# A hybrid retention and short-conv block on eight cores: prefix rows staged in an idle buffer, row norms in three steps, and an accumulation begun earlier

## The reference, cut to what matters

```
u = rmsnorm(x) * norm1_w * (1 + sc1) + sh1            # sh1, sc1, g1, ... from silu(c) @ w_ada + b_ada
q, k, v, og, cb, cc, cx, ga, gb = split(u @ w_in)
kh = rotary(k) / sqrt(128)
state_h = sum over earlier rows  gamma_h^(distance) * outer(k_row, v_row)      # retention, 4 heads
y_ret  = (silu(og) * groupnorm(retention(q, k, v))) @ w_ret_out
y_conv = (cb * causal_conv3(cc * cx)) @ w_conv_out
h = x + g1 * ((sigmoid(ga) * y_ret + sigmoid(gb) * y_conv) @ w_o)
out = rmsnorm(h + g2 * (relu(u2 @ w_ff1)^2 @ w_ff2))  # u2: second norm, as u
```

## Time and profile before

| | us |
|---|---|
| time, median of 3 runs (range) | 1362.46 (1361.74 to 1363.98) |
| the profiled execution's own time | 1362.84 |
| its span on the slowest core, core 3 | 1361.3 |
| spans of the eight cores | 1350.7 to 1361.3 |
| PE busy, share of the span | 1236.1, 91% |
| first group of the convolution branch begins (core 3) | 175.6 |

### The profile page before, as it was taken

One profiled execution on the slowest core, in us unless ns is written; L12 is line 12 of the kernel. 1 busy time (PEld: TensorE's weight loads), 2 busy tenths in 40 slices (PEclk: granted clock), 3 DMA queues, 4 the chain that ended last, 5 costly groups with the idle time before them and its releaser, 6 DMA issues.

```text
span 1361.3 us, 18923 instructions; the slowest of 8 cores (1350.7 to 1361.3 us)
## 1 busy us (share of the span) xinstructions
PE 1236.1 (91%) x6288; PEld 582.1 (43%) x6288; DVE 480.3 (35%) x907; ACT 421.1 (31%) x714; POOL 499.8 (37%) x513
## 2 busy tenths in 40 slices
PE   2467799999999999986999999599999999999997
PEld 0233354444444554543444444254444444444443
DVE  5345366766322366664002233260000252000045
ACT  1346143222211266666331112154330023331011
POOL 1155310000000377777653362126661125664012
PEclk8688899999999999997999999799999999999999
DMA  9779270240731500005447927987545449954423
GB/s 171 173 164 193 55 94 1 41 54 1 93 39 24 78 1 1 1 1 76 59 60 110 172 36 158 221 241 124 79 77 81 82 155 169 134 93 64 68 75 135
DMA packets 86591, 124.33 MB, mean 91 GB/s; under 512 B 4704, under 2 KB 69216, under 8 KB 86496
## 3 DMA queue, kind: packets, MB, share of 16 engines
q0 software_dynamic: 67632, 70.26, 37.5%
q1 hardware_dynamic: 16560, 44.48, 10.0%
q10 hardware_dynamic: 2304, 8.39, 1.8%
HBM read 176.59 MB, written 16.78 MB: 142 GB/s over the span
## 4 chain that ended last, share of the span: by engine, by line
PE 84%; DMA 7%; DVE 3%; POOL 2%; issue 2%; another core or an unknown queue 1%; ACT 1%; DVEq 0%; POOLq 0%; SPq 0%; ACTq 0%
PE PS L304 81%; DMA ring<-w_ada 3%; DMA h1s<-scr 2%; DMA scr<-brow 2%; PE PS L450 1%; DMA scr<-x_main 1%; DVE scr L871 1%; DVE scr L529 1%; PE PS L933 1%; DVE scr L527 0%; POOL ring L236 0%; POOL G_t L924 0%; POOL Z L555 0%; PE PS L858 0%
## 5 line engine op out<-in xcount | busy, mean ns | idle before, releaser
L304 PE MATMUL PS<-X,ring 128*128 128x512 bf16 x2560 | 568.3, 381 | 0.0
L304 PEld LDWEIGHTS PS<-X,ring 128*128 128x128 bf16 x2560 | 250.3, 98 | 300.8 <-issue 6.2
L304 PE MATMUL PS<-ring,Z 128*128 128x512 bf16 x896 | 212.5, 393 | 46.2 <-DVE G_t L422 14.7
L304 PEld LDWEIGHTS PS<-ring,Z 128*128 128x128 bf16 x896 | 88.7, 100 | 158.5 <-issue 64.1
L304 PE MATMUL PS<-Y,ring 128*128 128x512 bf16 x512 | 119.0, 379 | 1.8 <-DVE scr L765 1.8
L1116 ACT ACTIVATE scr<-PS 128x512 f32<-128x512 f32 x128 | 76.4, 597 | 140.8 <-PE PS L304 87.5
L304 PE MATMUL PS<-ring,X 128*128 128x512 bf16 x512 | 117.8, 379 | 0.0
L1135 DVE TENSOR_TENSOR AR<-PS,G_t 128x512 f32<-128x512 f32 x16 | 11.1, 692 | 295.1 <-PE PS L304 295.1
L304 PE MATMUL PS<-ring,Y 128*128 128x512 bf16 x512 | 113.4, 379 | 0.0
L757 ACT ACTIVATE scr<-PS 128x512 f32<-128x512 f32 x64 | 38.2, 597 | 187.4 <-PE PS L304 184.5
L236 POOL DMA_DIRECT2D ring<-w_in x17 | 16.7, 983 | 189.8 <-PE PS L304 189.8
(11 more groups left out here) (150 smaller groups left out, 1299.6 us busy)
## 6 DMA issues: line engine op xcount, KB each, us to landing
ring<-w_ff POOLq DMA_DIRECT2D x32, 1024.0 KB, 8.7
ring<-w_in POOLq DMA_DIRECT2D x17, 1024.0 KB, 22.6
scr<-x_main SPq DMA_DIRECT2D x32, 512.0 KB, 10.0
ring<-w_ada POOLq DMA_DIRECT2D x12, 1024.0 KB, 21.0
scr<-x_pre SPq DMA_DIRECT2D x16, 512.0 KB, 15.6
h1s<-scr SPq DMA_DIRECT2D x16, 512.0 KB, 7.3
scr<-h1s SPq DMA_DIRECT2D x32, 256.0 KB, 4.2
y<-scr ACTq DMA_DIRECT2D x16, 512.0 KB, 3.8
```

Of the source, the lines that this page charges most:

```text
L304: S.op("pe", lambda e: e.matmul(out, lhsT, rhs, start=start, stop=stop), reads=list(lkeys) + list(rkeys), writes=[okey])
```

## The change

- **Staging.** The first 6 tiles go to `scr0` to `scr5` as before. Tiles 6 to 13 go to the eight rows of X, which hold nothing yet (rows 0 to 3 had held the temporaries of the sine tables). From tile 14 on it is `scr` again.
- **Gates and order of the loads.** All prefix pairs come first, then all own pairs. Pair 2 waits for the fourth w_ada chunk (before: the third); pairs 3 to 7 are issued together, gated by the landing of the k weights. Behind them each scaling step issues one own pair.
- **Norms in three steps.** `pair_do(0)` squares, `pair_do(1)` variance and power, `pair_do(2)` scales; in the loop a pair's steps stand in three successive turns.
- **The loop** has 16 turns. Transposes are spread one or two calls to a turn; chunks 5, 6 and 7 are let go at t = 4, 8, 12 (before 2, 5, 8).
- **The tail.** Blocks 4 and 5 of M are begun in banks 2 and 3 with tiles 0 to 11, before the last tiles of `kd` are needed; the column sums come later; blocks 6 and 7 go last. The six evictions stand together behind the last norms.
- **O_load** no longer calls `load_x`: it takes `scr[t % 6]`. The counter of `load_x` stood at 32, so that before it began with `scr2`.

```
         def load_x(src, t, gate=()):
-            xi = xbuf["n"] % 6
+            i = xbuf["n"]
             xbuf["n"] += 1
-            dma("sp", scr[xi][:, :], src[t * 128:(t + 1) * 128, :], list(gate), SK(xi), ("xt", xi))
-            return xi
+            ap, keys = x_stage(i)          # X[:, (i - 2) % 8, :] for 6 <= i < 14, else scr
+            dma("sp", ap, src[t * 128:(t + 1) * 128, :], list(gate), keys, ("xt", i % 14))
+            return ap, keys
...
-        pairs = [("p", t) for t in range(0, 12, 2)] + [("m", 0), ("p", 12), ("m", 2), ("p", 14)] + [("m", t) for t in range(4, 16, 2)]
+        pairs = [("p", t) for t in range(0, 16, 2)] + [("m", t) for t in range(0, 16, 2)]
...
+        def pair_do(stage):
+            kind, t = pairs[n_next[stage]]
+            n_next[stage] += 1
+            (x_sq, x_rs, x_sc)[stage](kind, t)
+            if stage == 2 and n_next[2] + 2 > 7:
+                pair_load()
...
         s_wk, k_wk = ring_use()
+        for n in range(5):
+            pair_load([k_wk])
...
+        sq_at = (0, 1, 3, 4, 5, 6, 7, 9, 10, 12, 13)
+        for t in range(16):
+            p_k(t)
+            if n_next[2] < n_next[1]:
+                pair_do(2)
+            if n_next[1] < n_next[0]:
+                pair_do(1)
             if t >= 4:
                 p_m(t - 4, range(4), MA)
+            for kp in {2: (0, 1), 3: (2, 3), 5: (0,), 6: (1,), 7: (2, 3)}.get(t, ()):
+                p_tpart(1 if t < 4 else 2, kp, 2 + kp % 2, "act")
+            if g == 2:
+                p_tpart(3, i, 2, "act")
+            if t in sq_at:
+                pair_do(0)
+            if 10 <= t < 14:
+                m_tpart(0, t - 10, 3, "dve")
+            elif t >= 14:
+                for kp in (2 * t - 28, 2 * t - 27):
+                    m_tpart(1, kp, 2 + kp % 2, "dve" if kp % 2 else "act")
...
+        for t in range(12):
+            p_m(t, [4], [2])
+        norm_tail()
+        p_m(12, range(4), MA)
+        for t in range(12):
+            p_m(t, [5], [3])
+        norm_tail()
+        for t in range(13, 16):
+            p_m(t, range(4), MA)
+        for k, b in ((4, 2), (5, 3)):
+            for t in range(12, 16):
+                p_m(t, [k], [b])
...
         def O_load(t):
-            o_x[t] = load_x(x_main, t)
+            i = t % 6
+            dma("sp", scr[i][:, :], x_main[t * 128:(t + 1) * 128, :], [], SK(i), ("xt", i))
+            o_x[t] = i
```

More of the change, by code:

```diff
@@ L490, in x_load, with x_dst, x_src, x_sq @@
             x_of[kind, t] = load_x(x_pre if kind == "p" else x_main, t, gate)
-        def x_norm(kind, t):
+        def x_dst(kind, u):
+            return (xs_pre(u), xs_preK(u)) if kind == "p" else (mxs(u), mxsK(u))
+        def x_src(kind, u):
+            ap, keys = x_of[kind, u]
+            return (ap if kind == "p" else halves(ap)), keys
+        def x_sq(kind, t):
             col = t if kind == "p" else 16 + t
             for u in (t, t + 1):
-                xi = x_of[kind, u]
-                if kind == "p":
-                    sq_stats(scr[xi][:, :], SK(xi), xs_pre(u), xs_preK(u), col + u - t)
-                else:
-                    sq_stats(halves(scr[xi][:, :]), SK(xi), mxs(u), mxsK(u), col + u - t)
-            rs_stats(col, 2)
-            for u in (t, t + 1):
-                xi = x_of[kind, u]
-                if kind == "p":
-                    scale_x(scr[xi][:, :], SK(xi), xs_pre(u), xs_preK(u), col + u - t)
-                else:
-                    scale_x(halves(scr[xi][:, :]), SK(xi), mxs(u), mxsK(u), col + u - t)
+                src, sk_ = x_src(kind, u)
+                dst, dk = x_dst(kind, u)
+                sq_stats(src, sk_, dst, dk, col + u - t)
+        def x_rs(kind, t):
+            rs_stats(t if kind == "p" else 16 + t, 2)
+        def x_sc(kind, t):
+            col = t if kind == "p" else 16 + t
+            for u in (t, t + 1):
+                src, sk_ = x_src(kind, u)
+                dst, dk = x_dst(kind, u)
+                scale_x(src, sk_, dst, dk, col + u - t)
         def uT_ap(g, k):
@@ L627, in build_program @@
         ring_rel(k_wk)
-        for t in range(16):
-            mm(pa[0], ("pa", 0), ones_bf[:, :], ["ones"], kd_ap[t], [kd_key[t]], t == 0, t == 15)
         kbar = scr[6][:, 0:512]
-        S.op("act", lambda e: e.copy(out=kbar, in_=pa[0]), reads=[("pa", 0)], writes=[SH(6, 0)])
         MT = [scr[7 + k // 4][:, (k % 4) * 256:(k % 4 + 1) * 256].bitcast(BF16) for k in R8]
@@ L640, in m_evict, with norm_tail @@
                  reads=[("pa", b), SH(6, 1), ("mT", 0)], writes=[MTk[k]])
-        for k in range(4):
-            m_evict(k, MA[k])
-        MB = [1, 2, 3, 0]
-        for k in range(4):
+        def norm_tail():
+            if n_next[0] < len(pairs):
+                pair_do(0)
+            if n_next[1] < n_next[0]:
+                pair_do(1)
+            if n_next[2] < n_next[1]:
+                pair_do(2)
+        for t in range(12):
[10 more added lines that the diff above has]
+                p_m(t, [k], [b])
+        for t in range(16):
+            mm(pa[0], ("pa", 0), ones_bf[:, :], ["ones"], kd_ap[t], [kd_key[t]], t == 0, t == 15)
+        S.op("act", lambda e: e.copy(out=kbar, in_=pa[0]), reads=[("pa", 0)], writes=[SH(6, 0)])
+        norm_tail()
+        for k in range(6):
+            m_evict(k, (MA + [2, 3])[k])
+        for k, b in ((6, 1), (7, 0)):
             for t in range(16):
-                p_m(t, [4 + k], [MB[k]])
-            m_evict(4 + k, MB[k])
-            if k < 2:
-                pair_norm()
+                p_m(t, [k], [b])
+            m_evict(k, b)
+        while n_next[2] < len(pairs):
+            norm_tail()
         ring_open(len(chunks))
```

42 lines of the change are left out of this document (18 added, 24 removed).

## The result

| | before | after |
|---|---|---|
| median, us (range) | 1363.22 (1361.74 to 1365.47) | 1354.55 (1354.03 to 1355.31) |
| span of the slowest core | 1361.3 (core 3) | 1352.9 (core 4) |
| first `uTh` matmul there | 174.00 | 160.97 |
| from it to the output projection | 651.6 | 653.0 |
| the output projection until its last matmul | 82.2 | 85.4 |

The ratio is 0.9935 (95% 0.9918 to 0.9953): faster, by 8.7 us and not by the 29.5 forecast, and outside the range. On the slowest core 13.0 us are gained in the prelude, 1.4 lost behind it and 3.2 in the output projection; the rest, 453.5 us, is the same to 0.3.

What follows compares the result with a forecast made beforehand. The prelude was taken as bound by a chain of small waits and a late-starting DMA stream, not one full engine. Span 1361.3 - 33.7 (prelude) + 4 (output projection) = 1331.6 us; forecast 1333, range 1320 to 1349.

Steps and rivals of the forecast that it cites:

- The start: Prelude: k weights land at 48.5 us (bounds 46 and 52) for 59.35; `p_k(4)` starts at 65 for 77.08, gain 12.
- six tiles less are 12.3 us: Loads before the k weights: two prefix tiles beside them for eight, so 59.35 becomes 47.1 us.
- The pace: Loop of the k product: 3.4 us a turn where nothing is late; DVE's 3.7 us power wait removed at no new cost.
- the two stalls: Evictions behind own-row squares: `p_k(8)` at 83 to 84 for 78.6, `p_k(12)` at 102 for 97.
- The own rows: Loop's end: pair 13 lands at 114, squared at 116, PE free at 119; their stream a hair behind PE as next bound.
- rival C: Prelude: own rows' stream late, idle gaps or each late pair one chunk later; 1340 to 1348 us, chance 0.25.
- The tail: Before the convolution branch: 96 matmuls at 0.215 remain, 20.6 us; the branch starts at 140.3 for 174.00.
- 24 stand ahead, 5.2 us of the gain: Tail: of the 84 matmuls that stood behind the last decays, 24 now stand ahead, worth 5.2 us.
- The output projection: First load at about 827.4 us for 755.96; delay passes down stores, loads and `brow`: 4 us lost, bounds 0 and 16.
- Rival E: Prelude: only the start is gained (11 us), POOL and ACT eating the rest; 1355 us, chance 0.04.
- rival B: DMA in the prelude: x tiles flow beside chunks from the start, 10 us more gained; 1323 us, chance 0.2.
- the two signs of being wrong: Prelude: squares of prefix tiles wait past 72 us, or a chunk lands more than 30 us after its issue.

Runs made afterwards that it cites:

- run 9: Staging undone alone in the changed kernel (tiles through the six scratch buffers; three-step norms, loop and early blocks kept): 1361.8 us, ratio 1.001 to the kernel before.
- runs 4 and 6: Each against the changed kernel: 4 puts the three norm steps in one turn, 1360.3 us; 6 leaves out POOL's two rotation additions per k tile, 1347.2 us.
- Run 13: Changed kernel with old O_load order, masks and third chunk behind own rows, no early blocks; own tiles 8 to 15 load 128 of 1024 columns: 1337.9 us.
- run 15: Changed kernel with old O_load order, late masks, no early blocks, and the second chunk opened at turn 12, not 8: 1335.3, 1337.6 and 1342.6 us.
- Run 3: Changed kernel with own tiles 8 to 15 loading 128 of 1024 columns in the prelude: 1355.8 us in the profiled execution, cores 2 and 3 at clock 0.81.
- run 7: Changed kernel with the loads of kdec, qdec and mask and the third chunk opening put behind the own rows: 1347.6 us, ratio 0.990 to the kernel before.
- run 5: The changed kernel again, unedited, on another chip: 1352.3 us, ratio 0.993 to the kernel before.
- run 8: Changed kernel with blocks 4 and 5 of M not begun early: 1348.4 us, ratio 0.990 to the kernel before.
- run 1: Changed kernel with O_load on the buffers of before (scr2 first): 1359.9 us on the first chip, 1345.9 and 1348.3 on a second.

## Why the prediction was wrong

The direction and the places were right, the sizes weren't. Two steps failed, the pace of the turns and the landing of the own rows from tile 8 on; the start and the tail were mis-sized.

- **The start** ("48.5", "gain 12"): right in kind, 3.6 us late for the k weights (0.1 outside the bounds of 46 and 52), and the gain at `p_k(4)` is 4.8 (72.3 for 77.1) and not 12. The three steps take the wait for the power off DVE, not off PE: the transposes of group 1 wait 5.09 us for pair 3's scaling, whose power still stands on POOL behind two tiles' rotation. I had that scaling at 60; it ran from 64.15. The term "six tiles less are 12.3 us" isn't borne out either: without the staging the k weights come 2 us later (run 9).
- **The pace** ("turns go at 3.4 us", "at no new cost"): this step failed. The scaling, which had run while POOL was idle, now runs beside POOL's work, and each slows the other (runs 4 and 6): a turn takes 4.4 us. How much of the extra 1.0 is due to this and how much to the order of DVE's queue isn't priced; without POOL's two sums it is 4.1. The miss isn't seen at `p_k(12)`, which is late by 6.1 only, because the two stalls that I had put at `p_k(8)` and `p_k(12)` didn't come: no own row was waited for before 109. The first four own tiles, issued at 59 to 60, had landed by 77 when chunk 5 was issued, at 80.33 and not at 72, and the next four landed 5 us after their issue. Two errors offset each other there, which is luck. Run 13 shows the pace nearly bare: from the start of `p_k(4)` to that of `p_k(15)` 71.7 to 120.5 (medians), 4.4 us a turn with 3 to 5 us of late rows in all, where eleven turns at 3.4 are 37.
- **The own rows** (rival C, "1340 to 1348"): the step that failed most, 10.6 us between `p_k(12)` and the end of `p_k(15)`. Tiles 8 and 9, for which the sum had no wait, were issued just behind the second chunk and waited for 10.1 and 3.5 us; run 15 shows that the chunk does it. I had pair 13 (tiles 10 and 11) issued at 99, landed at 114 and squared at 116; it was issued from 111.55 on, since the scaling that frees its buffers came at the slower pace, and squared at 130.59 and 132.59, beside the third chunk and the mask. Run 3 prices the late rows at 10 us, run 7 chunk and three loads at 5.6 of them (median `uTh` 151.5 for 157.1 in run 5). This is the mechanism of rival C, each late pair one chunk later; its time was missed because start and pace were late as well. The slower pace also starves the stream: between 74 and 82 and between 90 and 98 the DMA queue of the rows is at a share of 0.36 and 0.27, as own pairs are issued only behind scalings.
- **The tail** ("20.6"): 23.5, with 13.26 for 48 matmuls. "24 stand ahead, 5.2 us of the gain" failed: they stand behind the last long wait and fill nothing (run 8).
- **The output projection** ("4 us lost"): right, 3.2 on the slowest core, 4.5 to 5.5 in run 1.
- **Rival E** ("only the start is gained", 1355, chance 0.04): its number is the measured 1354.55, by chance. Against it, the start gained 4.8 us at `p_k(4)` and not 11, and most of the gain came later: 7.9 at `p_k(8)`, 19.8 at `p_k(12)`, 13.0 at `uTh`. What it says of POOL is right in part.
- **DMA queues** (rival B): the own tile issued at 104 to 106 beside a fresh chunk landed after 19.6 us, with q0 at a share of 0.82 and q1 at 0.04 in that window, as in the earlier trace rows. So tiles don't flow beside a chunk from its start, and rival B had no part in the result.
- **The signs.** Neither of the two signs of being wrong came: the last wait of a square for a prefix tile ended at 61, and the chunks landed 11.5 to 25.5 us after their issue. No sign had been set on the pace of the turns or on own tiles 8 to 11, where the prediction failed.
- What stays open is the remaining scatter of 10 us between cores of one run, the clock behind PE's waits in the tail, and the clock of 0.81 on pairs of cores.

The sum of what was late against the forecast, on the slowest core: start 7.3, pace less the two absent stalls -1.2, own rows and what stands behind them 12.4, tail 2.2 (20.7 together).

## What to carry to other kernels

Moving an operation off a wait moves it beside other work: ask which engine is busy there, and price a VectorE operation like this scaling beside GpSimd at its slow figure (here 1.88 us for 1.42). In an in-order queue the last needed loads must stand ahead of those not yet needed; moving three loads and one chunk behind them gave 5 us, where the whole change had given 9. "Begun early" is early only if it stands ahead of the wait that it is to fill: look at the order of the engine, not at the program's intent.

## Of the hardware, unexpected

- Two scalings of 128x1024 on VectorE take 1.42 us alone and 1.88 to 2.44 beside GpSimd; GpSimd's 128x256 sum 0.72 alone and 0.98 to 1.10 beside them (core 4 of the changed kernel).
- Issues of three loads (2 KB, 2 KB, 256 KB) took 1.5 to 2.2 us each on SP while a chunk was under way (core 4 of the changed kernel), and 0.42 each in run 7, where the chunk's queue was at a share of 0.04 or less.
- A tile of 512 KB issued just behind a 1 MB weight chunk landed after 19.6 us, and after 5 us where no chunk was under way.
- On one of the four chips of the experiments, pairs of neighbouring cores ran at a granted clock of 0.81 for 133 to 162 us in all, in three of the four profiles taken there; what brings it on wasn't found.
